# Mixing attention one step deeper, with exponentials ahead of copies on ScalarE: a fused two-block kernel on one Trainium2 core

## The reference

```python
def diff_weights(q, k, v, lam):
    s = jnp.einsum('bqhmd,bkhmd->bhmqk', q, k).astype(jnp.float32) * (C_QK_DIM ** -0.5)
    p = jax.nn.softmax(s, axis=-1)
    w = (p[:, :, 0] - lam * p[:, :, 1]).astype(v.dtype)
    return jnp.einsum('bhqk,bkhd->bqhd', w, v)

def window_gqa(q, k, v, kc, vc, sink):
    ...
    p = jax.nn.softmax(jnp.concatenate([s_loc, s_ctx, s_sink], axis=-1), axis=-1).astype(v.dtype)
    ...
```

## Time and profile before

| | |
|---|---|
| median of 3 runs | 1549.24 us (1548.73 to 1551.07) |
| profiled execution, its own time | 1552.3 us |
| span of the profiled execution | 1549.1 us |
| TensorE busy | 1503.9 us |
| VectorE busy | 883.1 us |
| ScalarE busy | 710.5 us |

### The profile page before, as it was taken

The page is one execution under the profiler, slowest core; times in us unless marked ns, Lnnn a source line. Parts: engine busy times, 40 slices in busy tenths (PEclk is TensorE's granted clock), DMA queues, the critical chain, the costliest instruction groups (busy, mean ns, idle before and its releaser), DMA issues.

```text
span 1549.1 us, 23631 instructions
## 1 busy us (share of the span) xinstructions
PE 1503.9 (97%) x9911; PEld 1271.5 (82%) x9911; DVE 883.1 (57%) x1253; ACT 710.5 (46%) x1073; POOL 133.5 (9%) x157
## 2 busy tenths in 40 slices
PE   8999999999999999998999999999999998999998
PEld 6986997968888788646778888888878966899998
DVE  5633656566778669778363332333247868555554
ACT  5536553446666454567333212212236457443434
POOL 3002000010000346201100000000002400000000
PEclk9999999999999999889999999999999999999999
DMA  9478558598888652501523232323263350555551
GB/s 311 142 248 269 163 179 266 180 296 281 292 286 272 110 177 82 164 1 7 131 82 120 98 104 87 109 82 102 78 183 127 110 163 1 164 190 174 182 177 68
DMA packets 228945, 242.28 MB, mean 156 GB/s; under 512 B 13096, under 2 KB 222472, under 8 KB 228712
## 3 DMA queue, kind: packets, MB, share of 16 engines
q1 hardware_dynamic: 226704, 238.19, 48.2%
q0 software_dynamic: 1600, 2.37, 1.8%
q10 hardware_dynamic: 536, 0.22, 0.1%
HBM read 239.71 MB, written 1.05 MB: 155 GB/s over the span
## 4 chain that ended last, share of the span: by engine, by line
PE 87%; DVE 7%; ACT 3%; DMA 1%; issue 1%; SPq 1%; DVEq 0%; ACTq 0%
PE bank L818 18%; PE bank L820 18%; PE bank L819 18%; PE score_banks L1346 3%; PE bank L1380 2%; PE bank L2003 2%; PE bank L2010 2%; PE bank L2006 2%; PE bank L1363 1%; PE score_banks L952 1%; DVE small L1421 1%; DVE w_lo L807 1%; PE bank L917 1%; PE bank L919 1%; PE bank L918 1%; PE bank L844 1%
## 5 line engine op out<-in xcount | busy, mean ns | idle before, releaser
L807 DVE TENSOR_TENSOR w_lo<-raw,w_hi 128x2048 fp32r<-128x2048 f32 (+1 forms) x143 | 324.5, 2270 | 219.1 <-ACT w_hi L795 218.5
L818 PE MATMUL bank<-xn_hi,w_hi 128*128 128x256 f32 (+1 forms) x1216 | 401.8, 330 | 2.5 <-DVE w_lo L807 1.1
L820 PE MATMUL bank<-xn_hi,w_lo 128*128 128x256 f32 (+1 forms) x1216 | 398.9, 328 | 0.0
L819 PE MATMUL bank<-xn_lo,w_hi 128*128 128x256 f32 (+1 forms) x1216 | 398.9, 328 | 0.0
L795 ACT ACTIVATE w_hi<-raw 128x2048 fp32r<-128x2048 f32 (+1 forms) x143 | 269.6, 1886 | 127.3 <-PE bank L820 76.8
L818 PEld LDWEIGHTS bank<-xn_hi,w_hi 128*128 128x128 f32 x1216 | 231.4, 190 | 24.5 <-issue 2.2
L820 PEld LDWEIGHTS bank<-xn_hi,w_lo 128*128 128x128 f32 x1216 | 231.3, 190 | 20.0
L819 PEld LDWEIGHTS bank<-xn_lo,w_hi 128*128 128x128 f32 x1216 | 231.4, 190 | 19.8
L1850 DVE SCALAR_TENSOR_TENSOR xT<-bank,mod,xT 128x256 f32<-128x256 f32 x96 | 40.6, 478 | 119.7 <-PE bank L820 97.9
L818 PE MATMUL bank<-hid_hi,w_hi 128*128 128x256 f32 (+1 forms) x328 | 107.8, 329 | 0.6 <-DVE hid_lo L1111 0.6
L819 PE MATMUL bank<-hid_lo,w_hi 128*128 128x256 f32 (+1 forms) x328 | 106.9, 326 | 0.0
(11 more groups left out here) (472 smaller groups left out, 2664.3 us busy)
## 6 DMA issues: line engine op xcount, KB each, us to landing
raw<-in_w_ada SPq DMA_DIRECT2D x48, 1024.0 KB, 5.7
raw<-in_w_in SPq DMA_DIRECT2D x30, 1024.0 KB, 6.4
raw<-in_w_gate SPq DMA_DIRECT2D x22, 1024.0 KB, 5.4
raw<-in_w_up SPq DMA_DIRECT2D x22, 1024.0 KB, 5.3
raw<-in_w_exp_down SPq DMA_DIRECT2D x16, 1024.0 KB, 5.1
raw<-in_w_down SPq DMA_DIRECT2D x16, 1024.0 KB, 5.3
raw<-in_w_out SPq DMA_DIRECT2D x12, 1024.0 KB, 6.0
raw<-in_w_exp_up SPq DMA_DIRECT2D x10, 1024.0 KB, 8.9
```

The lines of the kernel that those rows point to most:

```text
L807: dve.tensor_tensor(w_lo[:, raw_slot[r], 0:k * cols], raw[:, raw_slot[r], 0:k * cols], high_half(name).bitcast(F32), ALU.subtract)\
L818: pe.matmul(o, s_hi, m_hi, start=i == 0, stop=False)
L819: pe.matmul(o, s_hi, m_lo, start=False, stop=False)
L820: last = pe.matmul(o, s_lo, m_hi, start=False, stop=i == n - 1)
```

## The change

In the mixing attentions the transposes of a unit are made three steps after its scores, not two, and its products four steps after, not three (`lag_of`). To hold the probabilities so long, there are six places for them instead of four; the two more lie in `rstd3`. Fox and cross keep their depth and their four places. In all four attentions ScalarE now does a step's exponentials before the step's copies. The loops are one step longer in the mixing attentions, and the pieces of work that stood at the first step behind the loop move with it.

```diff
-        NP_, NT = 4, 4
-        prob = lambda s: work[:, (s % NP_) * 512:(s % NP_) * 512 + 512]
+        NT = 4
+        MIX_FROM = mix_units[0][0]["s"][0]
+        lag_of = lambda units: 2 if units[0]["s"][0] < MIX_FROM else 3
+        prob_ring = lambda s: 4 if s < MIX_FROM else 6
+
+        def prob(s):
+            i = s % prob_ring(s)
+            return work[:, i * 512:i * 512 + 512] if i < 4 else rstd3[:, i - 4, :]
...
-            for i in range(len(units) + 3):
+            for i in range(len(units) + lag + 1):
...
-                if 2 <= i < len(units) + 2:
-                    unit = units[i - 2]
+                if lag <= i < len(units) + lag:
+                    unit = units[i - lag]
...
-                if i >= 3 and units[i - 3]["now"]:
-                    unit = units[i - 3]
+                if i > lag and units[i - lag - 1]["now"]:
+                    unit = units[i - lag - 1]
...
         def act_attention(act, units, fill=lambda i: None):
-            for i in range(len(units) + 3):
-                if 2 <= i < len(units) + 2:
-                    unit = units[i - 2]
+            lag = lag_of(units)
+            for i in range(len(units) + lag + 1):
+                if i < len(units):
+                    unit = units[i]
+                    act.wait_ge(*negmax_ready.at(unit["u"]))
+                    for s, sc in zip(unit["s"], unit["subs"]):
+                        if s >= prob_ring(s):
+                            act.wait_ge(*probs_turned.at(part_of_sub[s - prob_ring(s)]))
+                        nk = sc["nk"]
+                        last = act.activation(prob(s)[:, 0:nk], score_bank(unit, s)[:, 0:nk], ACT.Exp, bias=nmax(s),
+                                              accum_out=rsum(s))
+                        if "sink" in unit and s == unit["s"][-1]:
+                            last = act.activation(esink(unit["s"][0], 2), esink(unit["s"][0], 2), ACT.Exp)
+                        last.then_inc(*exp_ready.mark(s))
+                if lag <= i < len(units) + lag:
+                    unit = units[i - lag]
                     nk = unit["subs"][0]["nk"]
                     for p in unit["parts"]:
                         act.wait_ge(*probs_turned.at(p["p"]))
...
-                if i >= 4 and units[i - 4]["last"] and units[i - 4]["group"][0] in ("cross", "A", "D"):
-                    g = units[i - 4]["group"]
+                if i > lag + 1 and units[i - lag - 2]["last"] and units[i - lag - 2]["group"][0] in ("cross", "A", "D"):
+                    g = units[i - lag - 2]["group"]
...
-            moment, blocks, end = MIX_MOMENT[:, 0:ns * S], ns * ST, len(mix_units[l]) + 3
+            moment, blocks, end = MIX_MOMENT[:, 0:ns * S], ns * ST, len(mix_units[l]) + 4
...
-            for step in range(len(mix_units[l]) + 3, 60):
+            for step in range(len(mix_units[l]) + 4, 60):
```

More of the change, by code:

```diff
@@ L1335, in pe_attention @@
         def pe_attention(pe, units, fill):
-            ring, first = score_ring(units[0]), units[0]["s"][0]
-            for i in range(len(units) + 3):
+            ring, first, lag = score_ring(units[0]), units[0]["s"][0], lag_of(units)
+            for i in range(len(units) + lag + 1):
                 if i < len(units):
@@ L1394, in act_attention @@
                                        ACT.Copy).then_inc(*pT_ready.mark(p["p"]))
[L1395 to L1409, removed]
+                if i > lag and units[i - lag - 1]["last"]:
+                    g = units[i - lag - 1]["group"]
+                    act.wait_ge(*pv_done.at(units[i - lag - 1]["u"]))
                     act_group_out(act, g)
@@ L1414, in dve_attention @@
             own = Step(dve, dve_step)
-            for i in range(len(units) + 4):
+            lag = lag_of(units)
+            for i in range(len(units) + lag + 2):
                 if i < len(units):
@@ L1451, in dve_attention @@
                                .then_inc(*probs_ready.mark(p["p"]))
-                if i < len(units) + 3:
+                if i < len(units) + lag + 1:
                     fill(i)
```

## The result

The changed kernel takes 1561.61 us (median of 4 runs, 1558.41 to 1568.77), the kernel before, measured beside it, 1549.72 (4 runs, 1548.73 to 1551.07). The ratio is 1.0082, with an interval of 1.0065 to 1.0099: slower by 12 us, where +3.5 was forecast and 1559 was the end of the range. The profiled execution of the changed kernel is its slowest, 1568.77 us with a span of 1566.9 and a mean clock of 0.980; the other three had spans of 1556.7 to 1560.0 and clocks of 0.983 to 0.986, so this profile shows more loss than the median has.

The account below looks back on a forecast made before the run. TensorE, busy 97% of the span, was taken as the bound, so only its idle or low-clock time could be won. Fox 0.5, layer 0 0.9 and layer 1 2.1 made +3.5 us, 1552.7 from a median of 1549.24; range 1545 to 1559.

Parts of the forecast that it names:

- T(8): Layer 1 mixing attention, transposes of probabilities of unit 8, the first A unit: one wait of about 3 us.
- T(24): Layer 0 mixing attention, transposes of unit 24's probabilities: one wait of about 3 us, right after a weight half.
- T(13): Layer 1, transposes of unit 13: about 0.7 us wait where ScalarE's weight copy is ahead of the exponentials.
- V(12): Layer 1, unit 12's product with the values: 0.8 us wait for the group's low half, 1.13 before.
- so I price the C stretches at nothing: C units of the mixing attentions: VectorE sets the pace before and after, about 2.7 us a unit, so no cost.
- I take 0: Layer 0's first two thirds, where half-clock stretches decide: no change, with -3 and +2 us as bounds.
- S(8): Layer 1, scores of unit 8, the first A unit: start 22.0 us after the attention's first scores, 21.3 before.
- S(24): Layer 0, scores of unit 24, opening the last third: start 0.5 us earlier, then 43.7 us to the end.
- layer 1 +2.1: Layer 1's mixing attention: 64.7 us against 62.6, from laid-out work and waits in A and D units.
- layer 0 +0.9: Layer 0's mixing attention: last third 43.7 us against 42.3, less 0.5 for an earlier start.
- Rival 2: TensorE's clock falls once more in an A or D stage: 3.5 + 5 = +8.5 us, 1558; chance 0.17.
- Rival 3: Mixing attentions: earlier exponentials let scores run ahead, so late reductions never delay TensorE: 1543, half of it 1546; chance 0.21.

Follow-up runs that it names:

- e8: The changed kernel with VectorE's first weight half moved from the step with 7 units left to that with 4 left: 1559.02 us, ratio 1.0062.
- e11: The changed kernel run again, unaltered: 1565.05 us, ratio 1.0105 against the kernel before.
- e9: The changed kernel with modulation sums copied in step 3 and a finished group's low half ahead of VectorE's reduction: 1559.18 us, ratio 1.0055.
- e6: e1 plus modulation sums copied in step 3 and a finished group's low half ahead of VectorE's reduction: 1542.23 us, ratio 0.9946.
- e14: e10 with exponentials ahead of copies in the steps of A and D units only: 1559.09 us, ratio 1.0061.
- e10: e1 with the modulation's sums copied in step 3, VectorE's order as in the change: 1542.92 us, ratio 0.996.
- e1: The changed kernel with ScalarE's old order, copies ahead of exponentials, keeping depth and six places: 1552.59 us, ratio 1.001.
- e2: ScalarE's new order in all attentions at the old depth with four probability places: 1557.56 us, ratio 1.0052 against the kernel before.
- e12: e6 with the layer norm's product over the partitions, its scale and shift planned one step later: 1542.82 us, ratio 0.9956.
- e3: The changed kernel with three useless filler products, one in each of steps 1 to 3 of both mixing attentions: 1568.11 us, ratio 1.0122.
- e5: The changed kernel with ScalarE copying the modulation's sums in step 3, ahead of unit 4's exponentials: 1557.96 us, ratio 1.0056.

## Why the prediction was wrong

**Right: what waits, where, and how long.** The wait is handed on as laid out. T(8) in layer 1 and T(24) in layer 0 wait 3.24 and 3.00 us (about 3 forecast) for a copy behind exponentials behind a reduction behind a weight half; e8 moves that weight half and the waits shrink by 2.2 us. T(13) waits 0.70 (0.7), V(12) 0.61 (0.8), L974 2.22 in layer 1 and 1.40 in layer 0 (2 in both). The tails are 43.3 us in layer 1 (42.7 laid out) and 43.8 in layer 0 (43.7), and 43.4 and 45.1 in e11. Fox is 0.5 us longer (0.5).

**Wrong: the clock, which the sum of +3.5 us leaves as it was; in its terms, "so I price the C stretches at nothing", and for layer 0 "I take 0".** The waits and paces laid out for the C stretch are fair: in e11, where little time is lost to the clock ahead of S(8), S(8) comes 23.6 us after the start, and 1.7 of that is lost behind the L974 wait; without it 21.9, where 22.0 was laid out. What was left out is a lower clock. In layer 1 the 2.22 us wait at L974, which stood in the forecast, was costed as hidden by VectorE's pace; in the profiled execution half clock follows it, 6.9 us are lost in 13.7 us, and S(8) comes at 28.0 instead of 22.0. In layer 0 S(24) comes 67.7 us after the start, 62.1 forecast, with low stretches behind the waits of 1.40 and 1.35 us; one stretch lasts 24.3 us at 0.51. So the term "layer 1 +2.1" measured +8.7 (+4.4 in e11) and "layer 0 +0.9" +6.6 (+0.4 in e11), and most of the surplus is time lost at half clock. The prediction's own sign of being wrong, a clock below 0.9 in layer 1, came true in the first execution (0.88) and not in that of e11 (0.95). Fox's +0.5 and the two make 15.8 of the profiled execution's 17.8 us; the remaining 2.0 are in stages that the change does not edit: fox starts 1.4 us later, 1.6 come between fox and layer 0, and 1.0 is won between the layers.

**How much is clock, over all executions.** Every execution has its span and mean clock on record, and the span times (1 - clock) is an estimate of what it lost to the clock, good to about 1 us, since the clock has three digits. The medians are 12.4 to 13.9 us for the kernel before, 25.7 for the change and 31.3 in e11: 12 to 19 us more, where the change costs 12 and 15. So by this estimate the whole cost of the change is clock; the span times the clock, 1534.9 to 1535.4 us before, is 1535.0 in the change and 1532.0 in e11. In the same way e9 lost 23.4 and e6 9.2 (14 of the 17 us that the order costs), e14 24.1 and e10 11.6 (12.5 of 16.2), and e1 21.7 and e10 11.6 (all of the 9.7 us that the early sums earn). e2 lost 15.6 beside 13.9, so that at the old depth only 2 of 7 us are clock. The split is rough, because a TensorE at half clock also hides waits that would show at full speed.

**The nearest rival was placed too narrowly and made too small.** Rival 2, a further fall of the clock at 1558, had a chance of 0.17 and one fall of 5 us in an A or D stage. There are such falls behind the 3 us waits. In the change's first execution they are short (some 4 us, under 2 us lost in each layer); in e11's the one of layer 0 lasts 8 us at 0.57 (3.4 lost), and both layers' make the 5 us of the rival. Its price was fair, its 1558 still too low: 24 us were lost in the C stretches and the context's units ahead of S(24) and S(8) in the first execution, where the kernel before lost 11.9. The argument against it, "layer 1 never fell", was the flaw: one execution with a clock of 1.00 was taken for a property of the stage. Over the traces of the changed kernel and of the fourteen experiments layer 1 lost between 0 and 8.5 us. For the clause on the Trainium skill, "TensorE: Matmul & The Clock Gate", section "A second HAM failure mode: psum-queue depth-cycling": its rule is on frequent micro-idles, and I set it aside because of that one trace. The runs bear it out in part: kernels with fewer and shorter waits (e6, e10, e12) lose 1.7 to 3.4 us to the clock in layer 0 and nothing in layer 1. That many small ones are needed they do not bear out: in the change, in e3 and in e11 a fall directly follows one long wait.

**Rival 3 had the number of another kernel.** Depth alone does take the waits for normalised probabilities off the path: with the copies first, e1's tail in layer 1 is 1 us shorter. The "against" that I gave, the weight half ahead of the reduction, costs 3 us in the new order; with the copies first (e1) no such wait is left. With the early sums the gain is 7 us (e10), which is what rival 3 gave (1543), but by another edit than the one made and not by exponentials that start earlier, so that agreement is luck.

**What stays open.** Which wait brings the clock down, and for how long, was not settled. In these runs low stretches follow single waits of 1.35, 1.40, 1.92, 2.22, 3.00 and 3.24 us, but also 0.91 (e5), 0.53 in the kernel before at 643.2 and 0.43 in e6, and none follows 1.55 at T(9) before or 1.40 in the tails of e1, e6 and e10. The same wait of 2.22 us is followed by 13.7 or by 3.8 us of half clock. That the order and the late copy of the sums lower the clock is shown by single edits over all executions: 0.984 to 0.991 in e9 against 0.993 to 0.995 in e6, 0.979 to 0.989 in e1 against 0.990 to 0.995 in e10. That a fall is caused by the wait just ahead of it is not shown. The early sums take a wait of 1.12 us at 643.1 out of e1's layer 0, which no low stretch followed; the long low stretch that e10 does not have stands behind a wait of 1.43 us that both have:

```profile
669.75 1.05 PE L1387 MATMUL bank<-work,proj 128*64 128x128 f32 x8 [1.43 <-DVE xn_lo L1440]
```

```profile
670.00 0.66 PE L1387 MATMUL bank<-work,proj 128*64 128x128 f32 x8 [1.43 <-DVE xn_lo L1440]
```

(e1, then e10.) What brings it down at one place and not at another stays open; no run holds the waits fixed and changes the clock.

## What to carry to other kernels

When a pipeline is made deeper, look again at the order of each engine that works in program order: a copy that frees a bank is ready to go at once, an exponential waits for another engine, so the copy belongs ahead. With it behind, everything late on a third engine (here a 2.3 us weight half on VectorE) reaches TensorE through two queues. Where TensorE is full, do not price new waits at their length alone, hidden or not, and do not take one trace at a clock of 1.00 for a safe stage: here the two profiled executions of the changed kernel lost 27.3 and 15.3 us to half clock in the two mixing attentions, beside 17.2 and 18.7 us of waits there. And take apart a change of two halves before it is given up: depth, with one copy made a step earlier, was worth 7 us against the kernel before, the order beside it cost 17.

## What the runs showed of the hardware that was not expected

The granted clock of one and the same kernel differs between executions while its long waits agree to 0.01 us: spans of 1566.9 and 1555.8 us with mean clocks of 0.980 and 0.986, and 27.3 against 15.3 us lost in the two mixing attentions. In the first of them half clock began some 0.1 us before the wait ended: the first work behind the 2.22 us already took 1.02 us instead of 0.61 (in e11, 0.75). In the whole record the mean clock of one kernel moved between executions by up to 0.010 (e1: 0.979 to 0.989, with spans from 1558.1 to 1545.0 us). And three 128x512 products of no use, ahead of the wait, did not prevent the fall (e3: clock 1.00 in the 11.9 us ahead, 0.58 in the 8.1 us behind).
